# Issuing the bias spread of the next head pair from ScalarE, and four weight sums from GpSimd, in a two-branch gated mixer layer

## The reference

```python
h = rms_norm(x, pre_norm)
q, k, v, gate_a, u_b, v_b, gate_b, mg_a, mg_b = split(h @ w_in)
# A: every query attends to its own block of 128 keys and the one before it, with a sink
scores = einsum(q, band(k)) * HEAD_DIM ** -0.5        # 8 blocks of 128 queries per head
scores = where(mask, scores + bias, -1e30)            # bias = rel_bias[bucket(dist)], per head
probs = exp(scores - m) / (sum(exp(scores - m)) + exp(sink - m))
y_a = (einsum(probs, band(v)) * silu(gate_a)) @ w_branch_a
# B: gelu(u_b) * (tril(w_spatial) @ layer_norm(gelu(v_b)) + b_spatial)
y_b = (o_b * silu(gate_b)) @ w_branch_b
out = (sigmoid(mg_a) * y_a + sigmoid(mg_b) * y_b) @ w_out
x = x + rms_norm(out, post_norm)
```

## Time and profile before

| | |
|---|---|
| median of 3 runs | 917.24 us (915.69 to 918.41) |
| the profiled execution | 916.38 us, of which 914.6 us are the span of its instructions |
| PE busy | 898.6 us, 98% of the span |
| PEld, DVE, ACT, POOL busy | 82%, 73%, 55%, 55% |
| granted PE clock | 0.996 of full speed on the mean |
| DMA | 130.9 MB; SP's queue 129.42 MB in 170014 packets, ACT's 0.68 MB in 434 |
| spread of the bias by SP | 7 issues of 384 KB (and one by ACT) |

### The profile page before, as it was taken

How to read it: one execution, slowest core, us unless ns; L and a number is a source line. 1 busy time by engine, 2 the same in 40 slices (tenths; PEclk the granted TensorE clock), 3 DMA queues, 4 the chain that set the end, 5 groups by cost and what they waited for, 6 DMA issues and landing times.

```text
span 914.6 us, 12763 instructions
## 1 busy us (share of the span) xinstructions
PE 898.6 (98%) x4268; PEld 748.6 (82%) x4268; DVE 667.9 (73%) x1167; ACT 500.5 (55%) x982; POOL 501.1 (55%) x395
## 2 busy tenths in 40 slices
PE   9999999999999998999999999999999999999997
PEld 8888888888888786888788888888888888888886
DVE  6776794656666664756665679699689878989968
ACT  6654345676666675666566584335443534434563
POOL 3564236768687876677677857454552242042236
PEclk9999999999999999999999999999999999999999
DMA  8886655434434345534433354523379550435004
GB/s 302 201 200 160 228 173 133 127 103 119 114 102 118 105 126 152 166 101 114 120 97 103 116 161 138 189 92 116 92 254 366 184 207 1 135 102 224 1 1 183
DMA packets 170512, 130.90 MB, mean 143 GB/s; under 512 B 58552, under 2 KB 139472, under 8 KB 170320
## 3 DMA queue, kind: packets, MB, share of 16 engines
q1 hardware_dynamic: 170014, 129.42, 46.3%
q10 hardware_dynamic: 434, 0.68, 0.2%
HBM read 93.87 MB, written 39.35 MB: 146 GB/s over the span
## 4 chain that ended last, share of the span: by engine, by line
PE 60%; DMA 11%; DVE 9%; ACT 9%; issue 9%; SPq 2%; ACTq 0%; DVEq 0%; POOLq 0%; POOL 0%
PE acc L1025 19%; PE acc L1206 11%; PE acc L878 10%; DMA prob_d<-prob 9%; PE ps_m L1206 7%; PE ps_t L1206 7%; PE acc L968 2%; DMA turned_in<-prob_d 2%; SPq L664 2%; DVE neg_s L2143 2%; ACT prob L1584 2%; DVE gate L2109 2%; ACT prob L1576 2%; DVE ps_t L2140 1%; DVE pt_pack L2157 1%
## 5 line engine op out<-in xcount | busy, mean ns | idle before, releaser
L1025 PE MATMUL acc<-mv,w_hi 128*128 128x512 f32 x1344 | 350.6, 392 | 0.0
L1025 PEld LDWEIGHTS acc<-mv,w_hi 128*128 128x128 f32 x1344 | 246.3, 189 | 48.7 <-issue 2.6
L1025 PE MATMUL acc<-mv,w_lo 128*128 128x512 f32 x672 | 181.7, 392 | 0.0
L1819 POOL TENSOR_TENSOR w_lo<-sums,w_hi 128x1024 fp32r<-128x1024 f32 x48 | 117.7, 2456 | 73.1 <-ACT w_hi L1372 49.2
L1025 PEld LDWEIGHTS acc<-mv,w_lo 128*128 128x128 f32 x672 | 126.5, 188 | 27.9
L1819 POOL TENSOR_TENSOR w_lo<-raw,w_hi 128x1024 fp32r<-128x1024 f32 (+1 forms) x48 | 94.0, 1960 | 36.7 <-ACT w_hi L1365 29.6
L1206 PE MATMUL acc<-right,left 128*128 128x512 f32 x432 | 98.7, 389 | 0.0
L1576 ACT ACTIVATE prob<-neg_s,neg_max 128x129 f32<-128x129 f32 x128 | 50.5, 396 | 83.6 <-DVE neg_max L2143 83.0
L1206 PEld LDWEIGHTS acc<-right,left 128*128 128x128 f32 x432 | 81.0, 188 | 17.2 <-DVE left L2209 0.3
L2157 DVE TENSOR_TENSOR pt_pack<-turned_in,pt_pack 128x256 fp32r<-128x256 f32 x32 | 38.1, 1191 | 67.3 <-ACT pt_pack L1594 67.3
L1863 POOL TENSOR_SCALAR_AFFINE_SELECT pt_prev<-pt_pack 128x512 fp32r<-128x512 f32 x64 | 44.3, 693 | 68.2 <-DVE pt_pack L2133 34.5
(11 more groups left out here) (286 smaller groups left out, 1672.3 us busy)
## 6 DMA issues: line engine op xcount, KB each, us to landing
raw<-in_w_in SPq DMA_DIRECT2D x56, 512.0 KB, 4.8
ht_d<-sums SPq DMA_DIRECT2D x8, 512.0 KB, 4.8
mix_d<-mix_b SPq DMA_DIRECT2D x8, 512.0 KB, 3.7
prob_d<-prob SPq DMA_DIRECT2D x32, 128.0 KB, 2.2
turned_in<-prob_d SPq DMA_DIRECT2D x128, 32.0 KB, 2.2
ga_d<-gate SPq DMA_DIRECT2D x16, 256.0 KB, 4.1
tb<-tb_d SPq DMA_DIRECT2D x4, 1024.0 KB, 5.3
ub<-mix_d SPq DMA_DIRECT2D x7, 512.0 KB, 3.4
```

The costliest lines, as they stand in the source:

```text
L1025: ins = nc.tensor.matmul(bank, (w_lo if y == 2 else w_hi)[:, left + k * P:left + (k + 1) * P], right[:, (OPW if y == 1 else 0) + k * HALF: ...
L1819: nc.gpsimd.tensor_tensor(w_lo[:, c], src, w_hi[:, c].bitcast(f32), ALU.subtract).then_inc(wlo_ok, 1)
```

## The change

SP no longer issues the spread at k = 7 of each head pair. ACT issues the same DMA at k = 2, five steps earlier, behind norm(p, 1) and ahead of what step 2 has for ACT after attention. Its semaphore is the same, and load_bias waits for the same count at k = 11. The four sums for pair 17 move from DVE (steps 1 and 2 of pair 16) to POOL (steps 2 and 3 of pair 16).

```diff
@@ SP, attend(p, k)
-                if k == 7 and p + 1 < HEAD_PAIRS:
-                    sp.dma_start(*skew(p + 1)).then_inc(bias_out, 16)
                 if k == 11 and p + 1 < HEAD_PAIRS:
                     load_bias(p + 1)
@@ ACT, attend(p, k)
                 for blk in blocks_at(k, 0):
                     exps(p, blk)
+                if k == 2 and p + 1 < HEAD_PAIRS:
+                    act.dma_start(*skew(p + 1)).then_inc(bias_out, 16)
                 for blk in even_at(k, 5):
                     turned_hi(p, blk)
@@ POOL, after(n, s)
-                if s == 2 and n < FIRST_U:
+                if s == 2 and n <= FIRST_U:
                     left_sums_1(n + 1)
                 if s == 3:
                     left_lo(n, 4)
-                    if n < FIRST_U:
+                    if n <= FIRST_U:
                         left_sums_2(n + 1)
@@ DVE, after(n, s)
                 if s == 1:
-                    if n >= FIRST_U:
+                    if n > FIRST_U:
                         left_sums_1(n + 1)
@@
                 if s == 2:
-                    if n >= FIRST_U:
+                    if n > FIRST_U:
                         left_sums_2(n + 1)
```

## The result

The changed kernel takes 901.36 us (median of 4 runs, 900.58 to 901.52) beside 917.72 us (915.69 to 918.41) for the kernel before: a ratio of 0.982, 95% interval 0.981 to 0.984. The forecast was 902.0 us. Its profiled execution spans 899.8 us beside 914.6 us, so the two traces differ by 14.8 us and the medians by 16.4; the profiled execution of before was one of its quicker ones.

A forecast was written before the change was run, and what follows sets the result against it. It took PE, busy 98%, to lose time to late prob_d landings behind the spread in SP's queue. 6.8 + 3.8 + 3.5 - 0.6 + 1.0 = 14.5 us off 916.38 gave 901.9, stated as 902.0; 8 in 10 range 899.5 to 909 us.

The forecast's parts named there:

- (a): At k = 13, PE's six waits for the late block 4 go, with 0.15 us extra each: 6.8 us gained.
- (b): Between head pairs 3 and 4, the wait for late K and the half-pace matmuls behind it go: 3.8 us gained.
- (c): At k = 1 to 7 of six head pairs, the lag from ACT's in-order wait goes: 0.59 us each, 3.5 us.
- Rival 1: Relief is partial, lag or late K stays: 905.4 us without (c), 909.2 without (b) too; chance 0.17.
- The spread on ACT: At k = 2, ACT's issue is nearly covered, some 0.1 us late in six head pairs: 0.6 us lost.
- The traffic of the spread at k = 2: Two engines held while block 0's prob_back is under way, with 6.6 us to spare: cost 0.
- The sums: Pair 17's sums on POOL remove PE's 0.88 us wait in pair 16, plus 0.15: 1.0 us gained.
- 4: Where the spread is issued changes nothing, only the sums and SP's time remain: 915.4 us; chance 0.04.
- 2: The spread now holds up block 0, landing 0.8 us too late for ACT in seven head pairs: 907.6 us; chance 0.10.
- 3: ACT's issue isn't covered, 0.64 to 1.18 us in seven head pairs: 905.9 to 909.7 us; chance 0.07.
- 5: ACT's sequencer is blocked by the issue as SP's was, 4.34 us: slower, 924 us; chance 0.04.
- The signs: Expected in the profile: prob_d of k = 8 lands within 5 us, k = 13 waits and half clock near 354 us gone.

The follow-up runs named there:

- e5: Kernel before with the spread still on SP at k = 7 but written row by row, outer dimension 128 rows instead of two heads: 902.07 us.
- e11: Kernel before with the spread still on SP over two engines, but right behind prob_d of k = 8 instead of right ahead: 902.31 us.
- e8: Kernel before with only the spread of head pair 3 moved to ACT at k = 2, the other six left on SP: 912.23 us.
- e7: Changed kernel without the seven spreads, every head pair reading the bias rows of head pair 0: 900.63 us.
- e6: Changed kernel with the spread written row by row: 900.82 us.
- e2: Kernel before with only the sums of pair 17 moved to POOL, the spread left on SP at k = 7: 915.99 us.
- e9: Changed kernel with three small extra DMAs right behind the spread on ACT, four issues per head pair instead of one: 936.61 us.
- e3: Kernel before with the spread kept in SP's queue but moved from k = 7 to k = 2, sums left on DVE: 903.14 us.
- e4: Kernel before with the spread issued by ACT instead of SP, still at k = 7, sums left on DVE: 902.25 us.

## Why the prediction was right, point by point

- **What bounds the kernel.** Right: the landings were the loss, and with them gone PE is busy 99%. That the loss is that of standing behind a two-engine DMA is shown by e5 and e11, which keep everything but the shape or the order, and lose nothing. The 7.4 us were read too low: they are a landing (11.92) less the start of a reading back (4.50), and the landing itself goes down to 2.9 us, by 9.0. No term of the sum was worked out from them. That two engines did the work was an inference from a share of 0.13; e5 shows it.
- **(a) k = 13, 6.8 us.** Five gains read directly from the table (0.55, 1.03, 1.32, 1.81, 1.20) are each 0.25 to 0.27 us more than PE's wait at that place in the trace of before (0.29, 0.76, 1.05, 1.56, 0.95). I had 0.15. Head pair 3 with its wait of 1.31 us then makes 1.57, and the sum is 7.5 us.
- **(b) late K and half clock, 3.8 us.** From block 7 of head pair 3 to block 3 of head pair 4 the gain is 5.07 us; less 1.57 that leaves 3.5 us. e8 has it alone, 5.0 us with its k = 13.
- **(c) the lag, 3.5 us.** 0.63, 0.65, 0.65, 0.40, 0.66, 0.65 in head pairs 1, 2, 3, 5, 6, 7: 3.6 us. The small one stands behind V's wait. Rival 1 rested on this term coming from one odd head pair; it is in all of them.
- **The spread on ACT, -0.6 us.** 0: the issue isn't late by 0.1 us but early by 0.6. I had let the sequencer start when the reciprocal ends and took the worse of 0.64 and 1.18 us; it took 0.60 us. e7, without any issue, is ahead of e6 by 0.19 us, no more than the scatter.
- **The traffic of the spread at k = 2, 0.** This step failed. I looked at block 0 alone and asked who else waits for a DMA in that stretch only of K; once per execution V is reloaded two lines behind, at k = 3 of head pair 4. It lands 5.1 us later than before and costs 1.0 us in the table, 0.5 to 0.9 in the end. For block 0 the step held, but with less to spare than the 6.6 us that I gave it: the last of the four turned_in now lands after 8.0 us, at 413.4, and is needed at 414.53, so that 1.2 us are left.
- **The sums, 1.0 us.** 1.04 us in the table and in e2's trace, 1.15 us between the medians of e2.
- **The sum.** 7.5 + 3.5 + 3.6 + 0 - 1.0 + 1.0 = 14.6 us against 14.5 predicted and 14.8 between the spans. That the sum fits so well is luck in part: (a) was 0.7 us too low and (b) 0.3 too high, and the issue at 0.6 and V at 1.0 us cancelled but for 0.4. The forecast set out from the profiled execution of before (916.38), which was itself quick, and so came to 901.9 in place of 902.7 us. Between the medians 16.4 us were gained, 1.6 more than between the spans, nearly all because the median run of before was 1.3 us slower than its profiled one; where that run lost more isn't shown.
- **The rivals.** 4 is out by 14 us. 2 and 3 didn't happen. 5 didn't happen either, but e9 shows that its mechanism is real, and that the stop is as long as I took from SP's row (ACT stood still for 4.4 us): it needs a second DMA behind the spread in ACT's queue. Its price of 22.7 us would have been too low, since the half clock comes on top; e9 lost 35. What the prediction did not see is that the move wasn't needed at all: where the DMA is issued (e3, e11), from which queue (e4) and in which shape (e5) were each enough alone.
- **The signs.** prob_d of k = 8 lands within 4.4 us in all head pairs, and the others held too. I had looked for a new wait only at k = 7; the one that came, 0.76 us, stands at k = 6 of head pair 4.

## What to carry to other kernels

When one landing is long, look at what stands ahead of it in the same queue and at its outermost dimension before moving anything: here a DMA over two engines held up all that came behind it, and turning two dimensions of its pattern cost nothing that could be measured. Such a DMA may go to a compute engine's queue if it is alone there for as long as it drains; in e9 a second one behind it stopped that engine. And before a transfer is put into an idle stretch, list every DMA of that stretch in all repetitions, the ones that happen once included.

## What the runs showed of the hardware beyond that

- The issue of the DMA next behind a draining two-engine spread takes longer in every head pair of every trace that has one: 3.3 to 4.4 us for prob_d before, 1.9 to 2.9 for tb_d in e11, 1.1 to 2.4 for ta_d in e3, instead of 0.3 to 0.7, and 2.5 to 4.0 us on ACT in e9. Behind the row-wise spread prob_d takes 0.56 to 0.62 us. What the sequencer waits for in that time isn't shown.
- From another queue the same DMA isn't blocked (0.57 us) and lands after 7.4 us in place of 11.9.
- ACT's sequencer issued a DMA 0.6 us before the scaling that stands ahead of it in the program had started, and the activations went on without a gap.
- A wait of PE at k = 13 costs 0.25 to 0.27 us more than the row that shows it, in all five places where it could be read; the wait for V cost 0.24 us more (1.00 for 0.76), the one in pair 16 0.16 (1.04 for 0.88).
- The granted clock fell from the upper level to the lower after PE had waited 1.31 and 1.96 us within 6 us (before), after one wait of 3.12 us (e8) and after each of six of 3.27 to 4.23 us (e9), and not in head pair 5 of before, after one wait of 1.56 us.
